# A decoder trunk on one Trainium2 core: the work area and the buffer of squares moved up by 192 and 224 bytes

## The reference

```
for i in range(DEPTH):                       # 2 layers
    hn = rms_norm(h, mix_pre_g[i])
    if i % 2 == 0:
        m = gla_lru_mixer(hn, ...)           # linear attention + RG-LRU
    else:
        m = gdn_mixer(hn, ...)               # gated DeltaNet, 8 heads
    h = h + rms_norm(m, mix_post_g[i])
    c = mem_cross_attn(rms_norm(h, xa_pre_g[i]), rms_norm(mem, xa_mem_g[i]), ...)
    h = h + rms_norm(c, xa_post_g[i])
    f = sq_relu_mlp(rms_norm(h, mlp_pre_g[i]), mlp_w1[i], mlp_w2[i])
    h = h + rms_norm(f, mlp_post_g[i])
```

## The kernel before

| buffer | what it holds | offset modulo 512 before |
|---|---|---|
| hres, hresr, lin | residual stream, also summed operands of the MLP | 128 |
| act | normed activations, high and low | 128 |
| whi, wlo, wraw, slots 0 to 2 | blocks of weights | 128 |
| consts, masks, small | identity, ones, masks, small vectors | 128 (small 160, not moved) |
| work, workr and all that lies in it: tx, quads, staged, hid, memhl, khi, ksplit, qhi, vsplit, pth, spare | scratch of every stage | 448 |
| whi3, wlo3, wraw3: the fourth weight slot | blocks of weights | 448 |
| presum, xh_u, xl_u, xh_d, xl_d (EXTRA and inside work) | sums of weight blocks | 448 |
| sq, and the parts of xh, xl at SQ_AT | squares; sums of weight blocks | 416 |

## Time and profile before

### The profile page before, as it was taken

The page is one execution under the profiler, slowest core; times in us unless marked ns, Lnnn a source line. Parts: engine busy times, 40 slices in busy tenths (PEclk is TensorE's granted clock), DMA queues, the critical chain, the costliest instruction groups (busy, mean ns, idle before and its releaser), DMA issues.

```text
span 3021.7 us, 44776 instructions
## 1 busy us (share of the span) xinstructions
PE 2966.1 (98%) x16940; PEld 2420.1 (80%) x16940; DVE 2109.4 (70%) x2902; ACT 1445.8 (48%) x2651; POOL 834.0 (28%) x808
## 2 busy tenths in 40 slices
PE   8999999999999999999999999999999999999999
PEld 7788888887888778787888788878888788877876
DVE  8375638537788867778977666644754778886776
ACT  3435545336777612225433566644534667761112
POOL 3629300000566633330000112200000066663333
PEclk9999999999999999999999999999999999999999
DMA  6720331003566786533443323123101356687753
GB/s 214 250 91 22 109 122 49 29 28 132 194 245 244 276 308 244 208 112 129 153 151 138 102 60 115 52 71 112 42 29 35 147 196 243 244 290 280 251 202 133
DMA packets 198561, 457.33 MB, mean 151 GB/s; under 512 B 13792, under 2 KB 71408, under 8 KB 196464
## 3 DMA queue, kind: packets, MB, share of 16 engines
q1 hardware_dynamic: 159120, 414.32, 39.1%
q10 hardware_dynamic: 39264, 40.64, 3.9%
HBM read 304.96 MB, written 149.95 MB: 151 GB/s over the span
## 4 chain that ended last, share of the span: by engine, by line
PE 84%; DVE 9%; ACT 2%; DMA 2%; issue 2%; POOL 0%; ACTq 0%; DVEq 0%; POOLq 0%; SPq 0%
PE ps L3354 21%; PE ps L3584 10%; PE ps L3585 10%; PE ps L3586 10%; PE ps L3370 7%; PE ps L3824 3%; PE ps L3825 3%; PE ps L3826 3%; PE ps L3859 2%; PE ps L3753 2%; PE ps L3426 1%; DVE work L2158 1%; DMA wraw<-wstream_dram 1%; DVE hres L2189 1%; PE ps L3991 1%
## 5 line engine op out<-in xcount | busy, mean ns | idle before, releaser
L3354 PE MATMUL ps<-act,whi 128*128 128x512 f32 x2384 | 751.6, 396 | 3.1 <-DVE act L2179 2.8
L3354 PEld LDWEIGHTS ps<-act,whi 128*128 128x128 f32 x2384 | 444.1, 188 | 112.7 <-issue 11.1
L3354 PE MATMUL ps<-act,wlo 128*128 128x512 f32 x1192 | 466.8, 392 | 0.0
L2142 DVE TENSOR_TENSOR wlo<-wraw,whi 128x1024 fp32r<-128x1024 f32 x255 | 322.0, 1265 | 200.1 <-ACT whi L1143 165.9
L1023 POOL TENSOR_TENSOR stagedf<-quads 128x1024 f32<-128x1024 f32 x28 | 73.7, 2632 | 1062.3 <-ACTq L1434 1062.3
L2607 DVE TENSOR_TENSOR work<-work,ps 128x512 f32<-128x512 f32 x360 | 240.7, 684 | 139.5 <-PE ps L3586 137.7
L1495 ACT ACTIVATE whi<-wraw 128x1024 fp32r<-128x1024 f32 x112 | 115.9, 1057 | 380.5 <-POOL wraw L1042 317.5
L3354 PEld LDWEIGHTS ps<-act,wlo 128*128 128x128 f32 x1192 | 223.8, 188 | 49.3
L3584 PE MATMUL ps<-act,whi 128*128 128x512 f32 x624 | 246.8, 396 | 3.1 <-DVE work L2607 3.0
L3586 PE MATMUL ps<-act,wlo 128*128 128x512 f32 x624 | 245.0, 393 | 0.0
L1143 ACT ACTIVATE whi<-wraw 128x1024 fp32r<-128x1024 f32 x124 | 130.6, 1058 | 155.9 <-DMA wraw<-wstream_dram 152.9
(11 more groups left out here) (449 smaller groups left out, 7102.6 us busy)
## 6 DMA issues: line engine op xcount, KB each, us to landing
wraw<-wstream_dram SPq DMA_DIRECT2D x248, 512.0 KB, 3.6
hid_store<-staged SPq DMA_DIRECT2D x168, 512.0 KB, 3.4
act<-hid_store SPq DMA_DIRECT2D x36, 1024.0 KB, 11.0
hresr<-hid_store SPq DMA_DIRECT2D x56, 512.0 KB, 11.0
qkvz<-work ACTq DMA_DIRECT2D x32, 512.0 KB, 2.8
work<-qkvz ACTq DMA_DIRECT2D x64, 256.0 KB, 3.3
act<-hid_store SPq DMA_DIRECT2D x30, 512.0 KB, 11.5
presum<-wstream_dram SPq DMA_DIRECT2D x48, 256.0 KB, 4.5
```

The costliest lines, as they stand in the source:

```text
L2142: TT(wlo[s][:], wraw[s][:], whi[s][:].bitcast(F32), ALU.subtract).then_inc(w_split, 1)
L3354: last = mm(out_of(u)[:, 0:width], (wlo if hl else whi)[s][:, at:at + P], rhs(kt, xp, e), start=kt == hl == xp == 0, stop=kt == kts - 1 an ...
```

## The change

The start of the work area, and with it the fourth weight slot and everything that is placed relative to `WORK`, goes from 130,880 to 131,072, 192 bytes up. The buffer of squares `sq`, and the sums of blocks placed at `SQ_AT`, go from 128,800 to 129,024, 224 bytes up. With `base` at 1,152 all of them then start at 128 modulo 512, as act, hres and slots 0 to 2 do. No instruction is added, removed or moved on any engine, no DMA changes its size, and nothing else changes its place.

```diff
@@ -326,7 +326,7 @@
         UNIT = SEQ * 4
-        WORK = 130880
+        WORK = 131072
         hres = place("hres", 0, [P, KT, SEQ], F32)
         lin = place("lin", 0, [P, KT * SEQ], F32)
         act = place("act", 32768, [P, KT, 2, SEQ], F32R)
@@ -338,7 +338,7 @@
         small = place("small", 127520, [P, 320], F32)
-        sq = place("sq", 128800, [P, HALF], F32)
+        sq = place("sq", 129024, [P, HALF], F32)
         work = place("work", WORK, [P, 20, SEQ], F32)
@@ -358,7 +358,7 @@
-        EXTRA, SQ_AT = WORK + 20 * UNIT, 128800
+        EXTRA, SQ_AT = WORK + 20 * UNIT, 129024
```

## The result

| | before | after |
|---|---|---|
| median | 3021.69 us (4 runs, 3017.97 to 3026.5) | 2997.68 us (4 runs, 2994.7 to 2998.98) |
| ratio | | 0.9921, 95% interval 0.9907 to 0.9935 |
| profiled execution: span | 3021.7 us | 2997.2 us |
| its matmuls, busy | 2966.1 us | 2941.1 us |

One more run of the kernel before brought its median from 3024.7 to 3021.7. The change is worth 24.0 us, 0.79%; by the interval of the ratio it is between 19.6 and 28.1 us.

The account below looks back on a forecast made before the run. It took the pace of TensorE's matmuls as the bound: 20.0 us saved by agreeing offsets, less 0.8 for 256 columns and 1.4 for stalls, gives 17.8 us, from 3024.7 to 3007 us; range 2999 to 3019.

Parts of the forecast that it names:

- What bounds the kernel: Whole kernel: the time is the pace of TensorE, whose matmuls are busy 2966.1 of 3021.7 us.
- Agreement of offsets sets the pace: Matmuls whose two operands start at the same offset modulo 512 take 227 to 228 ns, others 233.3; chance 0.73.
- 3,704 matmuls at 5.4 ns, 20.0 us: Matmuls of 512 columns that disagree before and agree after, out of 10,656, save 20.0 us together.
- The agreeing matmuls: Matmuls whose operands already agreed before the change: nothing in the sum, about 2 us only in the largest case.
- Both ends: Largest and smallest outcome of the forecast: 24.9 us saved, 2999.8 us, and 10.8 us saved, 3014 us.
- Rival C: Partial gain: operands in work keep 229.2 ns or more, or only pure disagreement gains; about 9 us less, 3016; chance 0.12.
- Rival D: Slower: ScalarE and VectorE writing work at TensorE's offset cost matmuls 1.7 ns, 18 us, or twice that, 3043 us; chance 0.04.
- 256 columns, 0.8 us more: 288 matmuls of 256 columns, as in the keys of memory tokens, change to agreement at 2.9 ns more each.
- VectorE at 0: VectorE's additions, 691 to 692 ns at any offsets, don't see offsets and change the time by 0.
- Stalls take back 1.4 us: MLP turn from up to down: time saved on matmuls is waited for later at unchanged transfers, 1.4 us lost over both layers.
- DMA landings at 0: Transfers keep bytes and pieces, so 0 is taken; the bound is 4.4 us if two long landing waits grow a tenth.
- Rival B: Nothing changes: pace depends on which part of memory the operands lie in, below or above 128 KB; 3025 us, chance 0.11.

Follow-up runs that it names:

- exp. 2: Kernel after with squares and the sums at SQ_AT back at 128800, so only the work area moved: 2998.39 us, ratio to before 0.993.
- exp. 3: Kernel after with the work area 320 bytes further up, at 448 modulo 512 as before, squares still at 128: 3018.28 us, ratio to before 0.9996.
- exp. 4: Kernel after with work area and squares (and SQ_AT) both 512 bytes further up: 2999.7 us, ratio to before 0.9933.
- exp. 6: Kernel after with work area and squares (and SQ_AT) both 256 bytes further up: 2999.71 us, ratio to before 0.9927.
- exp. 7: Kernel after with work area and squares (and SQ_AT) both 192 bytes further up: 3012.76 us, ratio to before 0.9973.
- exp. 8: Kernel after with every buffer 384 bytes further up, large operands at 0 modulo 512: 2997.89 us, ratio to before 0.9916.
- experiment 1: Small kernel of TensorE alone, computation left out, 96 matmuls for each pair of offsets: 226.8 ns each agreeing, up to 233.3 ns disagreeing at 512 columns.
- experiment 5: Small kernel of TensorE alone, computation left out, 96 matmuls per sequence of offsets: one odd weights operand in 16 makes 21.88 us of 21.77, one odd moving operand 22.04.

## Why the prediction was wrong, step by step

I lined up the f32r matmuls of two executions, 11,376 in each, and compared the time from each start to the next start, in classes. Positive is time saved in us against the kernel before; each column is one profiled execution.

| class | count | after | exp. 2 | exp. 3 | exp. 4 | exp. 6 | exp. 7 | exp. 8 |
|---|---|---|---|---|---|---|---|---|
| 512 columns, disagreed before | 3,610 | 19.7 | 18.2 | 0.0 | 20.0 | 19.4 | 9.6 | 19.6 |
| 512 columns, agreed, among the 8 behind a disagreeing one | 2,642 | 8.9 | 8.9 | -0.1 | 9.0 | 8.7 | 0.6 | 8.7 |
| 512 columns, agreed, all others | 4,095 | 0.6 | 0.7 | -0.2 | 0.6 | 0.6 | -0.1 | 0.7 |
| 256 columns, disagreed before | 288 | -0.6 | -0.6 | 0.0 | -0.6 | -0.6 | 0.0 | -0.6 |
| intervals over 300 ns (stalls, other work between) | about 230 | -5.2 | -1.8 | 4.2 | -2.2 | -8.0 | -0.5 | -4.9 |

(The counts are those of the kernel after. Some matmuls stand before another line's work and are left out, so the first class is a little under 3,704. The intervals with other work between that aren't in the last row add 0.7 us in the kernel after; with them the five classes come to 24.0 us.)

- **What bounds the kernel: right.** The span fell by 24.5 us, the busy time of matmuls by 25.0.
- **Agreement of offsets sets the pace: right, in all but its length.** I counted in 512 bytes, as the change does; experiments 1 and 6 give 256. For this change the two are the same, since the differences of before (320, 192, 288 and 480) are no multiples of either.
- **3,704 matmuls at 5.4 ns, 20.0 us: right.** 19.7 us, 5.45 ns each. Experiments 4, 6 and 8, with other addresses and the same agreement, repeat it within 0.3 us.
- **The agreeing matmuls: wrong, and this is the step that failed.** They stand at nothing in the sum, and under *Both ends* I wrote that those next to disagreeing ones "give about 2 us more". They gave 8.9. Two readings went astray. I took the mixture of the earlier trace rows, 5.50 us, for operands in work that don't reach the full pace, made it the lower end of the range and the ground of rivals C and D; it was 16 agreeing matmuls held back by 8 others. And I counted 1,400 matmuls at 1.5 ns. By distance, nearly all of the 8.9 us lies in the 2,338 matmuls that are among the first six behind a disagreeing one, 3.8 ns each; the seventh and eighth give 0.1 us together. What I had before me said so: in the earlier trace rows six agreeing matmuls close behind disagreeing ones (the third to the eighth) took 1.37 us, 228.3 ns, in the earlier trace rows the agreeing block behind the disagreeing one 227.5, and in the earlier trace rows the long agreeing run 226.9. I read these as one value with some scatter. The surplus is of the kind that experiment 5 shows behind disagreement and behind a change of place; which of the two made how much of it in the whole kernel isn't told apart. After the change the blocks of the earlier trace rows take 226.7.
- **256 columns, 0.8 us more: right.** 0.6.
- **VectorE at 0: right for the time, and not quite for the row.** Lines by form after:

```profile
L2158 DVE TENSOR_TENSOR work<-work,sq 128x512 f32<-128x512 f32 x83 | 57.3, 690 | 69.0 <-ACT sq L1171 68.5
L2189 DVE TENSOR_TENSOR hres<-hres,work 128x512 f32<-128x512 f32 x72 | 49.2, 683 | 0.0
```

  The addition of hres and work went from 691 to 683 ns, the others stayed. 72 of 8 ns are 0.6 us, behind TensorE's backlog. It isn't the offsets: the row has 686 ns in experiments 2, 4, 6 and 8 and also in experiment 3, where hres and work lie at 128 and 448 as before. So the prediction's 0 stands.
- **Stalls take back 1.4 us: not settled.** The last row of the table is -5.2 us here, but it runs from -8.0 to +4.2 over executions whose pace is equal, and the third experiment, as slow as before, has +4.2. TensorE's idle time, summed over its gaps, went from 48.9 to 49.4 us. What is lost to stalls is below what one execution tells.
- **DMA landings at 0: right.** Experiments 4, 6 and 8 put the same transfers at other addresses without a difference in time; the median landings of the hidden blocks differ by tenths of a us between all executions.
- **Rival B, nothing changes, the area counts: out** by experiments 3 and 1. The second read port, by which the Trainium skill ("SBUF — State Buffer", section "A bandwidth-pool intuition that's wrong (but worth ruling out)") keeps a LDWEIGHTS and a moving operand apart, may be there, but the pace hangs all the same on where the two begin relative to each other: experiment 1 has 233.3 against 226.8 ns with nothing else running. The lines of 16 bytes that the same page gives (section "Door 1: The DMA port swizzle (why `[64,N]` ≈ `[32,N]`)") don't explain it either: with them alone a difference of 16, 32 or 64 bytes should cost nothing, and it costs the most.
- **Rival C, part of it: out.** The mixture of the earlier trace rows, in which tx lies in work, went from 5.50 to 5.44 us, so operands in work reach the full pace.
- **Rival D, slower: out.** After the change all operands begin where VectorE works too, and the three blocks of the MLP run at 226.7 ns each.

The time lies 9.3 us under the 3007 of the forecast. Of these 3.05 us are the new median of before, and 6.2 us are the larger gain: 8.9 and 0.6 us of agreeing matmuls that stood at nothing, against which the intervals over 300 ns took 5.2 us in the profiled execution where I had 1.4. These 6.2 us are no sharper than the measurement: the kernels whose operands agree gained 24.0 us here and 19.9, 21.2 and 23.0 us in experiments 4, 6 and 8 against their own runs of before, all more than 17.8.

Had the median of before stayed at 3024.7, the same gain would have given 3000.7 us, inside the range. That the largest end under *Both ends*, 24.9 us, comes near the measured 24.0 is luck: it has 6.4 ns for each disagreeing matmul, which gave 5.45, and 2 us for the agreeing ones, which gave 8.9.

Whether the load of weights and the stream of moving data hinder each other, in what way, and why the surplus outlasts its cause, isn't shown by these runs; only which addresses do it and what it costs.

## What to carry to other kernels

Where a tuned kernel is bound by a dense stream of fp32r matmuls with 512 columns, let stationary and moving operands begin at the same offset modulo 256 bytes, and all of them at one: it costs a padding of some bytes and gave 0.8% here. Other types weren't tried, and 256 columns lost a little. To find it in a profile, compare the time per matmul of equal units that differ in one buffer, by start times; the mean length in the lines (396 and 391 ns) hides it. And where single slow instructions sit in a pipelined stream, count what runs behind them as well: here 8.9 us stood beside 19.7.

## What the runs showed of the hardware

- With TensorE alone (experiment 1), the pace of fp32r matmuls with 512 columns depends on the start of the weights less the start of the moving operand, modulo 256: 226.8 ns at 0, 232.4 at 4 bytes, 233.3 at 16 to 64, 232.3 at 128, 229 at 192, 228.4 at 240 bytes (measured at 496). It isn't symmetric: 64 and 192, or 16 and 240, differ.
- The surplus outlives 24 disagreeing matmuls by six (231.7 ns each, experiment 5). One odd moving operand costs 45 ns in all, one odd stationary operand or one odd pair that agrees in itself 18 ns.
- Behind other work a run of agreeing matmuls starts slow as well: seven took 231.4 ns each in the kernel after, the later ones 226.7.
- With 256 columns it is the other way round by 2 ns: 119.9 ns agreeing, 117.8 with a difference of 320.
- VectorE's addition of 128x512 float32 took 683 to 692 ns in every execution and doesn't follow the offsets: that of hres and work took 691 ns before and 686 in experiment 3 with the same offsets modulo 512.
